# Four rotary additions moved from VectorE to GpSimd, and one ScalarE K copy moved ahead of an eviction, in a two-layer hybrid encoder

## The reference

```python
for l in range(DEPTH):                       # DEPTH = 2
    proj = h @ w_in[l]
    a_q, a_k, a_v, b_cq, b_ckv, b_kr, c_q, c_k, c_v = jnp.split(proj, IN_SPLITS, axis=-1)
    y_a = dilated_mixture(...)               # A: 4 heads of 64
    y_b = mla_attention(...)                 # B: 4 heads, 64 plain + 32 rotary columns
    y_c = axial_gqa(...)                     # C: 8 query heads over 2 K/V heads of 64
    ...

def mla_attention(cq, ckv, kr, ...):
    q = (rms_norm(cq, q_norm_g) @ w_uq)...   # per head 64 + 32 columns
    q = jnp.concatenate([q[..., :B_NOPE], apply_rope(q[..., B_NOPE:], ang)], -1)
    kv = (rms_norm(ckv, kv_norm_g) @ w_ukv)...
    k_rope = apply_rope(kr, ang)[:, None]
    ...
def apply_rope(x, ang):
    x1, x2 = jnp.split(x, 2, axis=-1)
    return jnp.concatenate([x1 * cos - x2 * sin, x1 * sin + x2 * cos], -1)
```

## Time and profile before

| | us |
|---|---|
| median of 3 runs | 1343.76 (1343.13 to 1343.97) |
| the profiled execution | 1341.76 |
| its span from first to last instruction | 1340.0 |
| TensorE busy | 1299.1 (97%) |
| VectorE busy | 972.2 (73%) |
| ScalarE busy | 603.3 (45%) |
| GpSimd busy | 317.2 (24%) |

### The profile page before, as it was taken

How to read it: one execution, slowest core, us unless ns; L and a number is a source line. 1 busy time by engine, 2 the same in 40 slices (tenths; PEclk the granted TensorE clock), 3 DMA queues, 4 the chain that set the end, 5 groups by cost and what they waited for, 6 DMA issues and landing times.

```text
span 1340.0 us, 19979 instructions
## 1 busy us (share of the span) xinstructions
PE 1299.1 (97%) x6888; PEld 1106.5 (83%) x6888; DVE 972.2 (73%) x1646; ACT 603.3 (45%) x1244; POOL 317.2 (24%) x428
## 2 busy tenths in 40 slices
PE   7998999999999999999999999999999999999996
PEld 5897797988878888888879977888897888888885
DVE  6779898867787867876674668997679456544678
ACT  4465889824323222212255668995263222221321
POOL 0041376603010110010030506774130010001005
PEclk9999999999999999999999999999999999999998
DMA  9774100142644664462224330010335333323322
GB/s 360 282 233 143 57 1 28 64 154 68 234 159 158 224 206 146 172 225 88 85 69 151 113 122 1 15 46 24 118 124 181 97 95 97 100 94 95 101 94 102
DMA packets 89217, 165.09 MB, mean 123 GB/s; under 512 B 8435, under 2 KB 19059, under 8 KB 89132
## 3 DMA queue, kind: packets, MB, share of 16 engines
q1 hardware_dynamic: 88980, 163.71, 36.7%
q10 hardware_dynamic: 152, 0.28, 0.1%
HBM read 161.84 MB, written 4.21 MB: 124 GB/s over the span
## 4 chain that ended last, share of the span: by engine, by line
PE 77%; DVE 12%; ACT 5%; DMA 3%; POOL 1%; issue 1%; SPq 0%; DVEq 0%; ACTq 0%
PE bank L1790 23%; PE bank L1792 22%; PE bank L1791 22%; PE bank L2070 4%; DVE ada_sum L1091 2%; DMA ada_b<-in_b_ada 1%; PE bank L2054 1%; PE bank L1729 1%; DMA slab_raw<-in_w 1%; DVE stats L1453 1%; DVE sqr L1436 1%; PE bank L2046 1%; PE bank L2045 1%; DVE ada_sum L1118 1%; DVE h_lo L1540 1%
## 5 line engine op out<-in xcount | busy, mean ns | idle before, releaser
L1790 PE MATMUL bank<-hT_hi,slab_hi 128*128 128x512 f32 (+1 forms) x640 | 236.6, 370 | 3.0 <-DVE qC L1306 3.0
L1792 PE MATMUL bank<-hT_hi,slab_lo 128*128 128x512 f32 (+1 forms) x640 | 235.4, 368 | 0.0
L1791 PE MATMUL bank<-hT_lo,slab_hi 128*128 128x512 f32 (+1 forms) x640 | 235.4, 368 | 0.0
L1532 DVE TENSOR_TENSOR slab_lo<-slab_raw,slab_hi 128x512 fp32r<-128x512 f32 x240 | 166.7, 741 | 86.8 <-ACT slab_hi L1035 64.6
L1790 PE MATMUL bank<-slab_hi,h_hi 128*128 128x512 f32 x512 | 200.5, 392 | 1.9 <-DVE slab_lo L1532 1.9
L1792 PE MATMUL bank<-slab_hi,h_lo 128*128 128x512 f32 x512 | 199.3, 389 | 0.0
L1791 PE MATMUL bank<-slab_lo,h_hi 128*128 128x512 f32 x512 | 199.2, 389 | 0.0
L1790 PE MATMUL bank<-slab_hi,hT_hi 128*128 128x384 f32 (+3 forms) x448 | 154.2, 344 | 7.9 <-DVE slab_lo L1194 4.5
L1792 PE MATMUL bank<-slab_hi,hT_lo 128*128 128x384 f32 (+3 forms) x448 | 151.5, 338 | 0.0
L1791 PE MATMUL bank<-slab_lo,hT_hi 128*128 128x384 f32 (+3 forms) x448 | 151.5, 338 | 0.0
L1790 PEld LDWEIGHTS bank<-hT_hi,slab_hi 128*128 128x128 f32 x640 | 120.6, 188 | 25.3 <-DVE qC L1306 5.6
(11 more groups left out here) (224 smaller groups left out, 2453.5 us busy)
## 6 DMA issues: line engine op xcount, KB each, us to landing
slab_raw<-in_w SPq DMA_DIRECT2D x256, 256.0 KB, 2.8
ada_w<-in_w_ada SPq DMA_DIRECT2D x42, 1024.0 KB, 7.3
slab_raw<-in_w_in SPq DMA_DIRECT2D x48, 192.0 KB, 4.6
slab_raw<-in_w_o SPq DMA_DIRECT2D x32, 256.0 KB, 2.7
boot_w<-in_w_ada SPq DMA_DIRECT2D x6, 1024.0 KB, 11.8
slab_raw<-in_w_in SPq DMA_DIRECT2D x16, 256.0 KB, 2.7
band<-bias_rows SPq DMA_DIRECT2D x8, 448.0 KB, 4.4
slab_raw<-in_w_in SPq DMA_DIRECT2D x16, 144.0 KB, 2.1
```

Source lines behind the costliest of these rows:

```text
L1532: dve.tensor_tensor(slab_lo[:, slot, :], slab_raw[:, slot, :], f32(slab_hi[:, slot, :]), ALU.subtract).then_inc(slab_lo_done, 1)
L1790: pe.matmul(dst, a_hi, w_hi, start=first, stop=False)
L1791: pe.matmul(dst, a_hi, w_lo, start=False, stop=False)
L1792: return pe.matmul(dst, a_lo, w_hi, start=False, stop=last)
```

## The change

GpSimd adds the two rotary products of the B heads' queries, in four instructions ahead of its work in attention, each followed by a wait for itself; VectorE no longer does it. ScalarE's first use of these queries waits for the new semaphore `q_roped`. And ScalarE makes the high part of the second K of C (`prepare_k(4)`) after the first of the two banks of B keys, no longer after the second. VectorE's counter of steps per layer falls from 252 to 251.

```diff
--- before.py
+++ after.py
@@ -312,6 +312,7 @@
         x_ready = sem("x_ready")
         ht_ready = sem("ht_ready")
 
+        q_roped = sem("q_roped")
         csq_done, cms_done, crstd_done, c_roped = map(sem, ("csq_done", "cms_done", "crstd_done", "c_roped"))
 
         bms_done, brstd_done, kr_roped = sem("bms_done"), sem("brstd_done"), sem("kr_roped")
@@ -624,6 +625,11 @@
                     inv_sqrt(rms[:, n % TT, j:j + 1], msq[:, n % TT, j:j + 1], 1, brstd_done)
                 if l == 0:
                     pool.sem_inc(x_ready, TT)
+                pool.wait_ge(evac_dve, l * D_LAYER + d_before("uk"))
+                for h in range(4):
+                    pool.tensor_tensor(qB[64:96, h, :], tmp[32 * h:32 * h + 32, 0, :], tmp[32 * h:32 * h + 32, 1, :],
+                                       ALU.add).then_inc(q_roped, 1)
+                    pool.wait_ge(q_roped, l * 4 + h + 1)
                 for u in range(UNITS):
                     p = prob[:, u % 4, :]
                     if affine_unit(l, u):
@@ -936,6 +942,7 @@
 
                 def prepare_q(i):
                     s, qs, at, _ = head_q(i)
+                    act.wait_ge(q_roped, l * 4 + HEADS[i][1] + 1)
                     act.activation(q_hi[at, s, :], qs[at, :], ACT.Copy).then_inc(head_hi, 1)
 
                 act.wait_ge(bank_ready, l * B_LAYER + ready_before("uq") + 4)
@@ -946,7 +953,8 @@
                     src = banks(JOB["uk"])[b]
                     act.activation(kB[0:64, 2 * b, :], src[0:64, :], ACT.Copy)
                     evac(kB[0:64, 2 * b + 1, :], src[64:128, :])
-                prepare_k(4)
+                    if b == 0:
+                        prepare_k(4)
                 for t in range(TT):
                     act.wait_ge(bank_ready, l * B_LAYER + ready_before("bv") + t + 1)
                     evac(vB[:, t, :], banks(JOB["bv"])[t][:, 0:256])
@@ -1345,15 +1353,6 @@
                     ins = dve.tensor_tensor(tmp[:, b, :], banks(JOB["uq"])[2 + b][:, :], ropeT[:, b, :], ALU.mult)
                     ins.then_inc(evac_dve, 1)
 
-                def rope_of_q(h):
-
-                    if h == 0:
-                        dve.wait_ge(evac_dve, l * D_LAYER + d_before("uk"))
-                    ins = dve.tensor_tensor(qB[64:96, h, :], tmp[32 * h:32 * h + 32, 0, :],
-                                            tmp[32 * h:32 * h + 32, 1, :], ALU.add)
-                    if h == 3:
-                        step(ins)
-
                 def v_src(i):
                     m, h = HEADS[i]
                     if m == "C":
@@ -1378,8 +1377,6 @@
                     dst = q_lo[at, s, :] if to is None else q_hi[to, s, :]
                     dve.tensor_tensor(dst, qs[at, :], f32(q_hi[at, s, :]), ALU.subtract).then_inc(head_ready, 1)
 
-                for h in range(4):
-                    rope_of_q(h)
                 prepare_k(0)
                 prepare_k(4)
                 for s in range(ATT_STEPS):
@@ -2186,7 +2183,7 @@
 
 
 
-DVE_STEPS = 252
+DVE_STEPS = 251
 
 
 def _tables():
```

## The result

The changed kernel takes 1344.85 us (median of 20 runs, 1343.37 to 1346.69), the kernel before 1343.08 us beside it (20 runs, 1340.51 to 1346.71). The ratio is 1.0013, with a 95% interval of 1.0007 to 1.0019: 1.75 us slower, by the interval 0.9 to 2.6 us. That is within the 0.2% called no difference; the forecast was 1345.2 us and 1.4 us. The profiled span is 1343.3 us, 3.3 us more than before. The change has no part in 1.84 us of this: VectorE's second rotary product, the last instruction ahead of the change, ends at 149.61 and not at 147.08+0.69 = 147.77.

A forecast was written before the change was run, and what follows sets the result against it. TensorE, busy 1299.1 of 1340.0 us, was taken as the bound, with VectorE's late K delaying attention's first maximum. Two layers at +0.7 us gave +1.4 us on the 1343.76 us median: 1345.2 us, range 1343.3 to 1347.3.

The forecast's parts named there:

- The sum: Whole kernel: first maximum +0.7 us later in each of 2 layers, +1.4 us in all, 0.1% slower.
- The additions leave VectorE: VectorE ahead of attention: the first K's low part starts at 149.19, not 150.61, winning 1.42 us.
- The second K's high part and the held tile: ScalarE's later B-keys eviction holds TensorE's fourth B-values tile; first score 1.30 us later, first maximum at least 0.18 us later.
- The additions' own length: GpSimd ahead of attention: each addition over 32 partitions takes 1.29 us, with 0.1 us allowed between them.
- signs of being wrong: Listed refutations: halves keep 0.7 us, tile not held, additions over 1.6 us, granted clock 0.50 clearly more or less.
- The turns: K low halves alternate with GpSimd's additions, 1.69 us a turn; first maximum +0.59 or +0.73 us, by who wins first.
- Rival 1: K low halves beside additions: turns cost nothing, the fourth tile decides, +0.18 us per layer, 1344.1 us; chance 0.24.
- The clock: TensorE behind the hole at attention's start: a low-clock stretch loses 1.7 us of work at 2.4 GHz.
- Rival 2: TensorE's ramp: a second low-clock stretch loses 1.7 us more per layer, 1348.6 us; chance 0.18 with dear additions.
- Rival 3: TensorE's ramp: a low-clock stretch goes away, returning up to 3.4 us in both layers, 1341.8 or 1340.7 us; chance 0.06.

The follow-up runs named there:

- e1: Kernel before with only ScalarE's second K moved ahead of the second bank of B keys, additions still on VectorE: 1343.97 us, ratio 1.0001.
- e3: Changed kernel with four GpSimd fills, which write SBUF but read nothing, in place of the four additions: 1343.82 us, ratio 1.0007.
- e2: Kernel before with only the additions moved to GpSimd, ScalarE's second K still behind both banks of B keys: 1346.54 us, ratio 1.0024.
- e4: Changed kernel with GpSimd's four additions moved into attention, ahead of units 33, 36, 39 and 42: 1346.66 us, ratio 1.0022.
- e7: Changed kernel with the second K's split moved into attention's ramp and three scores ahead of the fourth tile of B values: 1342.74 us, ratio 0.9994.
- e5: Kernel before with the second K's split moved into attention's ramp, at ScalarE's step 3 and VectorE's step 5: 1343.60 us, ratio 1.0007.
- e10: Kernel before with the second K's split moved to units 11 and 13 of attention, nothing else changed: 1343.83 us, ratio 1.0002.

## Why the prediction held, step by step

**The sum.** Predicted +0.7 us per layer, 1.4 us in all; at equal clock the last scaling is 0.69 and 0.67 us later, 1.36 us. The measured +1.75 us (0.9 to 2.6) holds it. The interval is wide: it would hold +0.9 us as well, so the time alone doesn't confirm the mechanism; the local times do.

**The additions leave VectorE.** Shown: the first low half starts 0.03 us behind its high part, and waits 1.44 us for it, as the step had it.

**The second K's high part and the held tile.** Shown by e1: +0.17 us for a floor of +0.18. The first score comes 155.62-149.61 = 6.01 us behind the product, before 152.48-147.77 = 4.71: 1.30 us later, as said. The hole at the tile was 1.06 us, not 1.2 to 1.3. It is counted from the end of the matmul ahead, 0.28 us long, while these matmuls start 0.12 us apart:

```profile
151.63 0.28 PE L1792 MATMUL bank<-u_hi,ckvT_lo 128*128 128x256 f32 x1
...
153.47 0.28 PE L1789 MATMUL bank<-u_hi,ckvT_lo 128*128 128x256 f32 x1
```

The first row is of before: the tile started at 151.75, 0.12 us behind it, so the 0.13 us behind the eviction weren't TensorE's delay in answering, as the prediction read them; in the changed kernel that delay is 0.06 us. The second row is of the changed kernel: 153.47+0.28 to 154.81 is the 1.06 us.

**The additions' own length.** 1.29 us for the undisturbed one, as taken, 0.07 us apart: adding over 32 partitions and writing at others costs what 128 partitions cost. The three disturbed ones took 1.60 to 1.83 us: stretched, as said, and not the longer additions of 1.60 us and more by themselves that the signs of being wrong meant.

**The turns.** Predicted +0.59 if the first half wins its race, +0.73 if addition 2 does; measured +0.63. In the trace addition 2 and half 1 both begin at 151.05, and the half ends in its normal 0.68 us, so the half had the way. The halves then end 1.70, 1.68 and 1.71 us apart (151.73, 153.43, 155.11, 156.82), the 1.69 assumed. The 0.04 us by which +0.59 was short are 0.02 of a later start (1.44 us behind the product, not 1.42) and 0.02 of the three turns (5.09 us, not 3 x 1.69 = 5.07). e1 (no additions), e3 (no reading) and e2 (tile not held) each show it from another side. Rival 1, no cost of the turns, would have ended at 6.68 us, and falls.

**The clock.** Here the price was mis-sized, though no term of the sum hung on it, and one of the prediction's signs of being wrong came: in both profiles of the changed kernel one layer had no 0.50 at all. Rivals 2 and 3 priced a low-clock stretch at its lost work, 1.7 us; the pair of profiles of the changed kernel gives 0.46 to 0.48 us. In the ramp TensorE waits for the exponentials, and I take it that most of the lost work lies in these waits; no run shows that by itself. Rival 3's event took place in one layer of two in both profiles of the changed kernel, and brought 0.5 us where 1.7 were priced. Rival 2's took place in e2 alone, where the single hole was 2.89 us: there +2.42 and +1.78 us per layer against before, +3.2 us in the measured time (1.0024). With ScalarE's order changed as well, TensorE is busy between two shorter holes, and no profiled layer had a second stretch.

**What isn't settled.** Why the clock fell in two of the changed kernel's four layers and not in the other two stays open: the holes are alike (1.06 and 1.19 us; 1.04 and 1.20 us). It is as open why it fell in e4's layer 0 and not in e1, though both have holes of 1.04 and 0.76 us there. Whether a kernel keeps its clock is known here from one or two profiled executions of each. The local terms explain all measured times within their intervals but one: e3's last scalings are 0.5 us in all earlier than before, and its ratio reads 0.4 us faster to 2.3 us slower. No version here is faster than the kernel before by more than its interval.

## What to carry to other kernels

Work that reads SBUF, moved from VectorE to an idle GpSimd, wasn't free here where VectorE had instructions with two SBUF inputs beside it: each pair took turns, 1.7 us from one to the next and not 0.7. Count how many such instructions stand between the moved work and the next wait that matters: with four the move lost, with two (e7) it won 0.45 us per layer by the profiles. One edit can take back part of another's price (here 0.40 us per layer), so run each alone and both together. A stall taken away ahead of the ramp (the start of attention, where the engines wait for each other unit by unit) came back in e5 to e10, where the work behind it was only moved inside: compare a point behind the ramp, not the first instruction in it.

## What the runs showed of the hardware that wasn't expected

- The same program lost its clock in layer 0 of one execution and layer 1 of another, at the same holes. One stretch at 1.2 GHz with 1.7 us of lost clock cost 0.46 to 0.48 us of time; with two in a row it was 1.87 and 1.26 us (e2 against e1, first maximum to last scaling), of which no run separates the clock from the one hole of 2.89 us.
- Four fills by GpSimd over 32x1536 took 5.67 us and didn't touch VectorE's subtractions of one SBUF tensor from another (1.40 us for two); four additions of 6.25 us over the same stretch made it 2.39.
- GpSimd's addition took 1.29 us over 32 partitions and over 128.
